# Attention scores of a fused transformer block from split keys and queries, and the modulation tiles one weight tile later

## What is computed

```python
sh1, sc1, gt1, sh2, sc2, gt2 = split(silu(c) @ w_ada + b_ada, 6)      # 12 tiles of 512 columns: ada0 to ada11
hx = rms_norm(x, norm1) * (1 + sc1) + sh1
qx = apply_rope(rms_norm(aq, q_norm), cos, sin)                       # 8 heads of 128
kx = apply_rope(rms_norm(ak, k_norm), cos, sin)                       # 2 heads of 128, 256 tokens + 256 of context
s = einsum('bhgqk', q_blk, k) * 128 ** -0.5
o = softmax(s) @ v                                                    # 8 heads x 2 tiles of 128 queries: 16 score tiles
x = x + gt1 * ((sigmoid(ga) * (attn @ w_br_attn) + sigmoid(gg) * (gla @ w_br_gla)) @ w_out)
x = x + gt2 * (relu((rms_norm(x, norm2) * (1 + sc2) + sh2) @ w_mlp1) ** 2 @ w_mlp2)
```

## Time and profile before

| what | value |
|---|---|
| median of three runs | 916.14 us |
| the profiled execution | 916.24 us |
| its span, first to last instruction | 914.3 us |
| PE busy | 889.6 us (97%) |
| DVE busy | 624.5 us (68%) |
| ACT busy | 479.6 us (52%) |
| memory read and written | 161.4 MB, 177 GB/s over the span |

### The profile page before, as it was taken

The page is one execution under the profiler, slowest core; times in us unless marked ns, Lnnn a source line. Parts: engine busy times, 40 slices in busy tenths (PEclk is TensorE's granted clock), DMA queues, the critical chain, the costliest instruction groups (busy, mean ns, idle before and its releaser), DMA issues.

```text
span 914.3 us, 14123 instructions
## 1 busy us (share of the span) xinstructions
PE 889.6 (97%) x5120; PEld 761.7 (83%) x5120; DVE 624.5 (68%) x1002; ACT 479.6 (52%) x759; POOL 11.3 (1%) x22
## 2 busy tenths in 40 slices
PE   6899999999999999999999999999999999999995
PEld 2688888887788887889999998897888999999984
DVE  2568779779777878776555558667777855555576
ACT  3647545665656566464444444444655744444453
POOL 0200000000000000000000000000000000000000
PEclk9999999999999999999999999999999999999998
DMA  9864212335346777636555557353434765555531
GB/s 359 335 184 170 80 55 93 97 111 170 131 144 224 250 254 247 211 134 235 190 192 187 184 184 262 106 184 121 156 115 162 227 222 207 191 186 188 194 102 47
DMA packets 45377, 162.11 MB, mean 177 GB/s; under 512 B 5616, under 2 KB 5760, under 8 KB 45329
## 3 DMA queue, kind: packets, MB, share of 16 engines
q1 hardware_dynamic: 42896, 155.73, 50.2%
q0 software_dynamic: 1296, 4.02, 1.6%
q10 hardware_dynamic: 1136, 1.70, 0.5%
HBM read 160.39 MB, written 1.05 MB: 177 GB/s over the span
## 4 chain that ended last, share of the span: by engine, by line
PE 83%; DVE 9%; DMA 3%; ACT 3%; issue 1%; SPq 0%; DVEq 0%; ACTq 0%
PE bank L691 70%; DVE w_lo L1675 3%; DMA raw<-in_stream 1%; PE bank L946 1%; PE bank L863 1%; DMA arena<-in_early 1%; PE bank L853 1%; PE bank L1147 1%; ACT w_hi L1245 1%; PE bank L961 1%; PE bank L966 1%; DVE act_lo L1675 1%; PE bank L870 1%; PE bank L884 1%; PE bank L811 1%
## 5 line engine op out<-in xcount | busy, mean ns | idle before, releaser
L1675 DVE TENSOR_TENSOR w_lo<-raw,w_hi 128x1024 fp32r<-128x1024 f32 x244 | 288.2, 1220 | 161.7 <-ACT w_hi L1245 161.3
L1245 ACT ACTIVATE w_hi<-raw 128x1024 fp32r<-128x1024 f32 x244 | 245.1, 1050 | 197.7 <-PE bank L691 165.1
L691 PE MATMUL bank<-w_hi,act_lo 128*128 128x512 f32 x720 | 292.9, 407 | 0.3 <-DVE w_lo L1675 0.2
L691 PE MATMUL bank<-w_lo,act_hi 128*128 128x512 f32 x720 | 281.3, 391 | 0.0
L691 PE MATMUL bank<-w_hi,act_hi 128*128 128x512 f32 x720 | 280.8, 390 | 0.0
L691 PE MATMUL bank<-act_lo,w_hi 128*128 128x256 f32 x640 | 183.0, 286 | 3.4 <-DVE act_lo L1675 3.0
L691 PE MATMUL bank<-act_hi,w_hi 128*128 128x256 f32 x640 | 181.1, 283 | 0.0
L691 PE MATMUL bank<-act_hi,w_lo 128*128 128x256 f32 x640 | 181.0, 283 | 0.0
L691 PEld LDWEIGHTS bank<-w_lo,act_hi 128*128 128x128 f32 x720 | 135.1, 188 | 29.4
L691 PEld LDWEIGHTS bank<-w_hi,act_lo 128*128 128x128 f32 x720 | 135.5, 188 | 27.3 <-issue 1.7
L691 PEld LDWEIGHTS bank<-w_hi,act_hi 128*128 128x128 f32 x720 | 135.6, 188 | 26.0 <-issue 1.2
(11 more groups left out here) (253 smaller groups left out, 771.3 us busy)
## 6 DMA issues: line engine op xcount, KB each, us to landing
raw<-in_stream SPq DMA_DIRECT2D x278, 512.0 KB, 4.4
arena<-in_early SPq DMA_DIRECT2D x14, 512.0 KB, 12.4
res<-in_x ACTq DMA_DIRECT2D x1, 1024.0 KB, 9.1
raw<-in_early SPq DMA_DIRECT2D x2, 512.0 KB, 13.6
arena<-in_ctx SPq DMA_DIRECT2D x1, 1024.0 KB, 13.3
res<-in_x POOLq DMA_DIRECT2D x1, 1024.0 KB, 8.2
arena<-in_norm_final POOLq DMA_DIRECT2D x1, 512.0 KB, 3.9
arena<-in_ple_b POOLq DMA_DIRECT2D x1, 512.0 KB, 5.3
```

The source lines that it names most:

```text
L691: last = pe.matmul(o, left, right, start=start and m == 0, stop=stop and m == 2, skip_group_check=shared)
L1245: return act.activation(o, i, ACT.Copy)
L1675: return dve.tensor_tensor(o, x, hi.bitcast(F32), ALU.subtract)
```

## The change

1. The scores are three split products (`product`) instead of one f32 matmul. Queries are held as high and low parts in `act_hi` and `act_lo`, columns T to 2T of their head, where the head's output replaces them later; keys of one head as `key_hi` and `key_lo` in two small buffers. `q_t` is gone.
2. At the turns ACT takes the high part of every block but the second key head, which it copies, and DVE the low part after it. PE's waits follow: score 0 waits for three low parts, score 2 for five.
3. A new step ("keys", 1), behind item 7, replaces the first key head's parts by the second's: ACT after score 7, DVE after ACT, and score 8 waits for it.
4. Turn 1 stands, as before, behind item 0, but one part later. go0 has no modulation tile; ada7, 8, 9, 4 and 5 stand in go1, ga1, wba0, wba1 and gg0.

```diff
--- before.py
+++ after.py
@@ -251,13 +251,13 @@
     gs = [("gstate", j) for j in range(6)]
     p.woven("aq1", [gs[0], k[2], gs[1], k[3], gs[2], k[4], gs[3], q[0]])
     p.woven("ga0", [gs[4], q[1], gs[5], None, q[2], ("qkturn", 0), q[3]])
-    p.woven("go0", [None, att[0], ("qkturn", 1), att[1], None] + att[2:6], ada=7)
-    p.woven("go1", att[6:14], ada=8)
+    p.woven("go0", [None, att[0], None, ("qkturn", 1), att[1]] + att[2:6])
+    p.woven("go1", att[6:8] + [("keys", 1)] + att[8:14], ada=7)
     out = out_steps()
-    p.woven("ga1", att[14:] + [("gosilu",), ("sigmoid", "ga0"), ("explog",), ("gomul",)], ada=9)
-    p.woven("wba0", out[:9], ada=4)
-    p.woven("wba1", [("sigmoid", "ga1"), ("explog",)] + out[9:18], ada=5)
-    p.woven("gg0", out[18:] + [("merge", "gla", h, 5) for h in range(2)])
+    p.woven("ga1", att[14:] + [("gosilu",), ("sigmoid", "ga0"), ("explog",), ("gomul",)], ada=8)
+    p.woven("wba0", out[:9], ada=9)
+    p.woven("wba1", [("sigmoid", "ga1"), ("explog",)] + out[9:18], ada=4)
+    p.woven("gg0", out[18:] + [("merge", "gla", h, 5) for h in range(2)], ada=5)
     p.woven("gg1", [("merge", "gla", h, 5) for h in range(2, 4)] + [("sigmoid", "gg0")], ada=10)
     p.steps += [("sigmoid", "gg1"), ("explog",)]
     y = [("yturn", i) for i in range(4)]
@@ -425,7 +425,7 @@
         kv = slots(7, 2).rearrange("p (t n) -> p t n", t=4)
         k_t = slots(9).rearrange("p (h t) -> p h t", h=KVH)
         q_in = tiles2(10)
-        q_t = slots(12, 2).rearrange("p (h t) -> p h t", h=QH)
+        key_hi, key_lo = (s[:, 0:2 * T] for s in (small_hi, small_lo))
         prob = slots(14, 2)[:, 0:3 * NC].rearrange("p (b k) -> p b k", b=3)
         prob_t = slots(14, 2)[:, 3 * NC:4 * NC].rearrange("p (c q) -> p c q", c=4)
         go_x = tiles2(10)
@@ -507,9 +507,12 @@
                 return mo[:, :, j * NC:(j + 1) * NC]
             return ga_half[j] if n[:2] == "ga" else gg_x[:, :, j * NC:(j + 1) * NC]
 
-        def qk_target(n):
-
-            return k_t[:, n, :] if n < 2 else q_t[:, 2 * n - 4:2 * n - 2, :].rearrange("p h t -> p (h t)")
+        def qk_parts(n, bank):
+
+            if n == 0:
+                return key_hi, key_lo, bank[:, :]
+            h = slice(2 * n - 4, 2 * n - 2)
+            return act_hi[:, h, T:2 * T], act_lo[:, h, T:2 * T], bank[:, :].rearrange("p (h t) -> p h t", h=2)
 
         def keys_queries(h):
 
@@ -553,6 +556,7 @@
             sem("turned"), sem("turn_y_dve"), sem("turn_y_act"), sem("turn_hi"), sem("turn_done"))
         roped, qkt_done, qkt_act, qkt_dve = (sem(n) for n in ("roped", "qkt_done", "qkt_act", "qkt_dve"))
         q_sq = sem("q_sq")
+        keys_hi, keys_lo = sem("keys_hi"), sem("keys_lo")
         score_done, nmax_ready, exp_done, prob_ready = (
             sem("score_done"), sem("nmax_ready"), sem("exp_done"), sem("prob_ready"))
         pt_done, pt_evac, ot_done, ot_hi, ot_lo = (
@@ -827,8 +831,10 @@
                     pe.wait_ge(gs_copy, GH)
                 pe.wait_ge(roped, 2 + part)
                 for n, bank in QK_BLOCKS[part]:
-                    if n >= 4:
-                        pe.wait_ge(qkt_act, n - 3)
+                    if n == 4:
+                        pe.wait_ge(qkt_dve, 1)
+                    if n == 5:
+                        pe.wait_ge(qkt_act, 2)
                     for m in range(4):
                         if n < 2:
                             source = kv[:, m, n * HD:(n + 1) * HD]
@@ -844,14 +850,15 @@
                 if i < N_ATT:
                     h, t = i // TT, i % TT
                     if i == 0:
-                        pe.wait_ge(qkt_act, 4)
+                        pe.wait_ge(qkt_dve, 3)
                     if i == 2:
-                        pe.wait_ge(qkt_act, 5)
-                        pe.wait_ge(qkt_dve, 1)
+                        pe.wait_ge(qkt_dve, 5)
+                    if i == N_ATT // KVH:
+                        pe.wait_ge(keys_lo, 1)
                     if i >= 2:
                         pe.wait_ge(exp_done, i - 1)
-                    pe.matmul(psum[4 + i % 2][:, :], q_t[:, h, t * P:(t + 1) * P], k_t[:, h // (QH // KVH), :],
-                              start=True, stop=True).then_inc(score_done, 1)
+                    product(psum[4 + i % 2][:, :], (key_hi, key_lo), (act_hi[:, h], act_lo[:, h]),
+                            slice(T + t * P, T + (t + 1) * P), slice(0, 2 * T), True, True).then_inc(score_done, 1)
                 j = i - 3
                 if 0 <= j < N_ATT:
                     h, t = j // TT, j % TT
@@ -1617,9 +1624,16 @@
                     if step[1] == 0:
                         act.wait_ge(gx_qin, GH)
                     for n, bank in QK_BLOCKS[step[1]]:
-                        if n < 5:
-                            act.wait_ge(qkt_done, n + 1)
-                            act.activation(qk_target(n), psum[bank][:, :], ACT.Copy).then_inc(qkt_act, 1)
+                        act.wait_ge(qkt_done, n + 1)
+                        if n == 1:
+                            act.activation(k_t[:, 1, :], psum[bank][:, :], ACT.Copy).then_inc(qkt_act, 1)
+                        else:
+                            hi, _, turned_block = qk_parts(n, psum[bank])
+                            hi_part(hi, turned_block).then_inc(qkt_act, 1)
+                elif kind == "keys":
+                    act.wait_ge(qkt_act, 2)
+                    act.wait_ge(score_done, N_ATT // KVH)
+                    hi_part(key_hi, k_t[:, 1, :]).then_inc(keys_hi, 1)
                 elif kind == "att":
                     attention(step[1])
                 elif kind == "yturn":
@@ -2327,9 +2341,13 @@
                     (rope_keys if step[1] == "k" else rope_queries)(step[2])
                 elif kind == "qkturn":
                     for n, bank in QK_BLOCKS[step[1]]:
-                        if n == 5:
-                            dve.wait_ge(qkt_done, n + 1)
-                            dve.tensor_copy(qk_target(n), psum[bank][:, :]).then_inc(qkt_dve, 1)
+                        if n != 1:
+                            dve.wait_ge(qkt_act, n + 1)
+                            hi, lo, turned_block = qk_parts(n, psum[bank])
+                            lo_part(lo, turned_block, hi).then_inc(qkt_dve, 1)
+                elif kind == "keys":
+                    dve.wait_ge(keys_hi, 1)
+                    lo_part(key_lo, k_t[:, 1, :], key_hi).then_inc(keys_lo, 1)
                 elif kind == "att":
                     attention(step[1])
                 elif kind == "yturn":
```

## The result

The changed kernel takes **926.13 us** (median of 4 runs, 925.04 to 926.86) against 916.21 for the kernel before on the same chip: ratio 1.0104, interval [1.0091, 1.0116]. It is slower by 9.9 us; 920.0 was forecast, with 923.5 as the upper end of the range. The profiled execution, the slowest of the four, took 926.86 us with a span of 925.1, 10.8 more than the span before.

What follows compares the result with a forecast made beforehand. PE was taken to set the time, with DVE's queue nearest to stopping it in the attention. Scores -2.9, turns +4.3, second key head +0.9, modulation tiles +1.5 gave +3.8 on 916.24: 920.0 us, range 917.0 to 923.5.

Steps and rivals of the forecast that it cites:

- The scores, -2.9: Sixteen attention scores on PE: three split products take 0.68 instead of 0.86 us each, 2.9 us less, all counting.
- nothing is booked for it: The switch between split products and f32 only moves from ahead of the score to behind it, so no cost.
- The turns, +4.3: Turn 1 in go0: PE waits 1.2 (rope), 2.3 (score 2), 1.8 us (probabilities), less 1.0 us: +4.3 us.
- the old wait: PE's 1.0 us wait at 232.99 in go0, on the attention output's low part, was to go.
- Second key head, +0.9: In go1, score 8 waits for the second key head's parts: +0.9 us, bounds 0 and 1.5.
- items 12 and 13: Attention items now back to back: wait bounded at 0 to 1.0 us, taken as 0 because DVE is not behind.
- The modulation tiles, +1.5: gg0 to half of wbg0: ada5 adds 6.4 us of DVE work, delaying ada10's sum: +1.5 us, bounds 0.8 and 6.4.
- Packed without a gap: DVE from 323.96 to 351.20: 28.0 us of work in 27.24 us, so 0.8 us late if it never idles.
- Rival (c): DVE falls behind for good in gg0 and gg1, up to 6.4 instead of 1.5 us: 922 to 925; chance 0.13.
- The clock, 0: The forecast sum had no term for a fall of PE's granted clock.
- Rival (d): After go0's waits, 10 us of products at 1.2 instead of 2.4 GHz cost 5 us: 925; chance 0.03.
- the row: Trace record of products starting 0.23 us apart beside the scores, used instead of the skill's 216 ns: saving 2.9 us.

Runs made afterwards that it cites:

- ada7_early: Changed kernel with go0's roundings and cuts later, ada7 moved to aq1, other modulation tiles placed as in the kernel before: 916.53 us.
- late_rounds: Changed kernel with three of go0's four weight roundings and cuts postponed behind turn 1: 920.77 us.
- merge_early: Changed kernel with the last steps of heads 2 and 3 in gg1 moved ahead of roundings that wait for their units: 926.15 us.
- mod_alone: Kernel before, with f32 scores and its own turns, only the modulation tiles one tile later: 920.82 us.
- x_late: Changed kernel with POOL's 1 MB reload of x issued only when the first y is ready: 926.41 us.
- awake: Changed kernel with four f32 products of a constant, results overwritten, ahead of PE's sum for ada10: 925.10 us.
- awake_turns: Changed kernel with one, two and one f32 products of constants where PE waits in go0, results overwritten: 924.12 us.
- gg0_empty: Changed kernel with go0's roundings and cuts later, no modulation tile in gg0, ada5 in gg1 and ada10 in wbg0: 923.62 us.
- late_mod_back: Changed kernel with go0's roundings and cuts later and the modulation tiles back where the kernel before had them: 920.64 us.

## Why the prediction was right or wrong

The direction was right, the size was not: +3.8 forecast, +9.9 measured.

- **The scores, -2.9.** In a steady item the step is right, 3.40 instead of 3.58 us, and most of it counts: the changed kernel has 2.5 us less work on PE, ada7_early 2.4. What failed is "nothing is booked for it", said of the switch: of two items back to back the second saves nothing (2.17 against 2.18 us), because there the split products have f32 work on both sides. That is 0.4 us of the error.
- **The turns, +4.3.** 1.2, 2.3 and 1.8 were forecast; from start to start, as the forecast counts, 1.3, 2.4 and 1.7 came, and the old wait, 1.15 so counted, is gone: 4.2. The replay of the three queues held, and late_rounds shows its cause.
- **Second key head, +0.9.** Listed as 0.9, 1.15 from start to start. The trace shows no wait at items 12 and 13, so 0 was right as well.
- **The modulation tiles, +1.5.** This is the main step that failed: waits of 4.6 us (0.7 for ada5's sum, 3.9 for ada10's), 4.9 from start to start, three times the term, inside the bounds of 0.8 to 6.4 given with it. "Packed without a gap" was the wrong end to take: DVE works 16.2 of 20 us there. ACT stands behind transfers (3.2 and 1.5 us), a hi part stands behind ACT's roundings, DVE behind the hi part (2.0 us), and ada10's units land late for DVE as well (0.3 and 1.3). That they land late because DVE releases buffers late is argued, not measured; in merge_early DVE does not wait for ada10's last three units. mod_alone shows that the moved tiles bring this by themselves (4.3 us of waits with f32 scores and the old turns). merge_early takes 2.2 of the 3.9 away and x_late 0.9, in one profile each; how the rest divides is open. Rival (c), given 0.13, was the nearer description.
- **The clock, 0.** The second step that failed. Rival (d) had a chance of 0.03 and was dismissed because a wait of 5.3 us at the start left the clock full. It fell twice, for 1.7 + 1.6 = 3.3 us: 3.5 us at half clock each, at two places, not 10 us at one. With PE kept at work at its place (awake, awake_turns) each fall was absent, in one profile each; its cost is read from the products' distance, 0.42 instead of 0.23 us.

The sum by what was measured: -2.5 + 4.2 + 1.2 + 4.9 + 3.3 + 0.1 (the next norm's transposes wait 0.6 instead of 0.4) = +11.2, less 0.4 for a start that was earlier in this execution (208.17 against 208.53 at turn 0): 10.8, as the spans differ. The medians differ by 9.9.

The granted clock of the kernel before was not full "from end to end" either: the last slice of the earlier trace rows says 8, and in the last 4 us, with PE out of work, it is 0.50.
The Trainium skill (TensorE: Matmul & The Clock Gate, What's actually happening) says that an idle array falls back to half its clock; "here no stretch shows it" was said of it. The end of the kernel before shows it, at no cost, and the changed kernel shows it where it costs, with products 0.42 us apart instead of 0.23. The Trainium skill's figure for issue (TensorE: Matmul & The Clock Gate, Back-to-back issue gap), by which the saving would have been 3.4 us, moves further from what was measured than the row did.

## What to carry to other kernels

Where one engine is nearly always busy, price a block of work that moves by who stands behind it in the in-order queues of its helpers; where buffers are released late, don't assume that their gaps will be filled. A new wait of a few microseconds on TensorE deserves a real chance of a clock fall on top of its length (here 1.6 to 1.7 us each). Before making work cheaper on the bounding engine by adding steps to its helpers, look whether moving one unrelated block into a helper's gaps is worth more: here that alone gave 1.2 us, and the cheaper scores gave nothing on top. And count a wait from start to start, not from the end of a record: here each cost some 0.15 to 0.3 us more than its listed length.

## What the hardware showed that was not expected

- The clock's fall does not follow the longest wait alone. PE's wait of 5.2 us at the start leaves it full; 2.1 and then 1.5 us (225.3 and 227.8) are followed by the fall (0.83, 0.83 in the two windows); behind the wait for ada10's sum or a turn of y it fell in the changed kernel (3.9 us), gg0_empty (3.7), awake_turns (3.6) and mod_alone (3.2), and stayed in x_late (3.0), late_rounds (2.8) and merge_early (1.7), as behind late_mod_back's wait for ACT (2.7). These are one execution each. The same wait can go either way: 1.3 us at 38 us was followed by a fall in merge_early (0.71 from 40 to 45) and by none in the changed kernel. After the same waits in go0 the depth differed from execution to execution, 0.83 and 0.83 in the changed kernel, 0.72 and 0.60 in merge_early.
- A product behind f32 work takes 0.32 us to the next one where 0.23 is the rule, whatever it belongs to (232.18 to 232.50 for a score). With that and the 0.38 us behind the last one, three products between f32 work are as dear as one f32 product of two records.
